# A hybrid attention/RNN decoder layer on 8 cores: gate weights and the first RNN chunk moved across the q,k,v boundary, attention and gating spread over the dense units

## The chip, the cores and the metric

The kernel runs on 8 cores (NeuronCores) of one Trainium2 chip. Each core computes one of the 8 batch elements; the cores exchange nothing. The metric is device time in microseconds of the slowest core. Cores 0 to 3 lie on one die, cores 4 to 7 on the other.

## The reference

One decoder layer, batch 8, 4096 tokens, width 1024, float32 in and out:

```python
h = RMSNorm(x); z = h @ W_in      # q,k,v (512 each) | x_rnn | y_rnn | g_attn | g_rnn (1024 each)
A = moba_attention(q, k, v)       # 8 heads of 64, QK-norm, relative bias,
                                  # own causal block of 256 keys + the top-3 past blocks by q . mean(k)
B = rg_lru(conv1d(x_rnn)) * gelu(y_rnn)
x = x + W_out(sigmoid(g_attn) * (A @ P_attn) + sigmoid(g_rnn) * (B @ P_rnn))
x = x + W_2(relu(RMSNorm(x) @ W_1) ** 2)    # hidden width 4096
```

In the recurrence each channel keeps h_t = a_t h_(t-1) + sqrt(1 - a_t^2) * i_t * conv_t, where a_t and i_t come from two block-diagonal matmuls.

## The kernel before, in words

**Order of the work.** Nothing is issued directly. Helpers `op` (line 461) and `dma` (line 466) append an operation with a modelled cost to a program object `Prog`; afterwards its `schedule` takes, for each engine in turn, the ready operation that comes first in program order, and writes one fixed order per engine. The order in which the Python code calls the helpers is therefore the priority, and tile names (buffers) give the waits. Every compute row of the profile has line 461, every DMA row line 466, so rows are told apart by tile names. PE is the matmul engine, DVE, ACT and POOL do the elementwise work, SP issues the ordinary DMAs. A DMA issued by POOL can convert f32 to bf16 on the way; these are the rows on the queue "software_dynamic".

**Stage A, q,k,v.** 32 tiles of 128 tokens. `FEn(t+1)` normalises a tile and transposes it (`s_hb` to `s_hT`, stored to HBM as `h_s`), `FEm(t)` does 24 matmuls of 128x512 against `s_wqkv`, `FEq(t)` does the QK-norm (`s_ssq` on POOL, `s_qa`, `s_ktm`) and stores q, k, v. From t = 4 one load per tile is taken off the list `wB`, all on POOL's queue with a cast: `wx`, `wy` (8), `wbda`, `wbdi`, then `wga`, `wgr`, `wpr` (12 loads of 512 KB in bf16).

**Stage B, the RNN.** 8 chunks `s` of 512 tokens, each in two halves `g` of four channel tiles. `RNN(s,g)` does 16 matmuls per channel tile with `s_wx`, `s_wy` ("xy"), copies the x half out of PSUM into `s_xr` (ACT), and runs the 4-tap convolution as one ACT and three DVE operations into `s_cv`, then POOL casts to `s_cvb`. The three tokens before the chunk come from a tile `halo`: DVE copies them in and out, two copies of 128x3 per channel tile. `RNN2(s,g)` does the gate matmuls `s_wbda`, `s_wbdi` ("ai"), tanh and exp on ACT, then on POOL the square of a and min(.,1) times -0.25 (a tensor_scalar in place on `s_rr`), the square root on ACT, then products and the scan on DVE, and POOL writes `s_orn`. `GATE1(c,m)` does for one of eight tiles of 128 output channels 8 matmuls each with `s_wga`, `s_wgr` and `s_wpr`, and stores two f32 tiles `t_s` and `rm_s`; four calls for chunk s-1 stand in each half of chunk s. `WCAST` turns two MLP weight slabs per half into bf16 in HBM.

**Stage C.** `QLOAD(c)` loads q of chunk c; `GM(c)` makes, for four tiles of 128 queries, the block mask (matmuls `s_kmBD,s_qp`, top-3 by `s_top`, a transpose of `s_maskb`, then eight small DMAs from `s_mskT` into `s_qT`). `attention(c)` is a list of units, one per head and 128 keys: an S matmul `s_qT,s_kTr` into a PSUM bank, an exp on ACT into `s_PT`, four small matmuls `s_Vr,s_PT`; then transposes into `s_oT`. Attention of chunk 0 alternates with the eight `GATE1(7,m)`. Everything else is a list `dense`: `gating(c)`, eight units of four matmuls `s_oT,s_wpa`, each multiplied (DVE) by the stored gate tile, which SP loads into `s_t1r`, and added to `s_rmr` into `s_mT`; `outproj(c)` with `s_mT,s_wo` and the residual `s_x1T`; and `W1`, `W2` in two halves, `s_h2T,s_wsl` and `s_uT,s_wsl`. `marks[c]` is the position of `gating(c)` in `dense`. The units of `attention(c)` are put among the dense units from `marks[c-1]` to `marks[c]`; `QLOAD(c)` and all of `GM(c)` stand together at `marks[c-1]`. There are two buffers each of `s_t1r` and `s_rmr`.

## Time and profile before

| | us |
|---|---|
| median of 3 runs | 2646.11 (2641.7 to 2646.79) |
| the profiled execution | 2649.26 |
| span of its slowest core, core 3 | 2647.7 |
| spans of the eight cores | 2624.2 to 2647.7 |
| granted TensorE clock, mean of core 3 | 0.953 |

The profile is of core 3. Stage A runs to about 276 us, stage B to about 890 us, attention of chunk 0 to about 1050 us, and the rest is the dense list with attention of chunks 1 to 7 in it. A row of the windows view reads: start and end, length, then for PE, PE's weight loads, DVE, ACT and POOL the busy time (and the number of instructions), then the granted clock of TensorE, the mean busy share of the 16 DMA engines, and GB/s. A clock of 1.00 in these rows is 2.4 GHz; 0.50 would be 1.2 GHz all the time. A row of groups reads: line, engine, operation, out<-in, shapes, count, then busy time and mean ns of one, then the idle time just before them and what ended it. "<-" in a waits row is the thing waited for.

### The profile page before, as it was taken

How to read it: one execution, taken by the hardware profiler on the slowest of the kernel's cores; microseconds unless marked ns; L12 is line 12 of the kernel's file. 1: busy time of each engine (PE TensorE's matmuls, PEld its weight loads, DVE VectorE, ACT ScalarE, POOL GpSimd, SP SyncE). 2: the span in 40 equal slices, each digit the busy share in tenths (PEclk: the TensorE clock that was granted, in tenths of full speed). 3: DMA queues.
4: the chain of work that ended last, by engine and by line, in shares of the span. 5: the costliest groups of instructions: out<-in, count | busy, mean ns of one | idle time of the engine just before them, and what ended most of it. 6: DMA issues, size and time to landing. Idle time of an engine off the chain costs nothing.

```text
span 2647.7 us, 43842 instructions; the slowest of 8 cores (2624.2 to 2647.7 us)
## 1 busy us (share of the span) xinstructions
PE 2369.7 (90%) x14810; PEld 1131.8 (43%) x14810; DVE 1093.7 (41%) x1946; ACT 1287.8 (49%) x2313; POOL 729.4 (28%) x593
## 2 busy tenths in 40 slices
PE   4888689999999776989989989989998998999799
PEld 2444333444444332434434434534543553555344
DVE  3767775866776523233233132133123213211332
ACT  2444666666666523332434434535654664676111
POOL 3665565665565401011011011011001101100110
PEclk9998899999999887999989989999998998999899
DMA  7998555653112445454445455445444544453443
GB/s 189 214 219 168 104 88 128 116 117 93 59 67 72 111 143 161 140 162 163 144 150 180 134 158 150 140 139 163 152 144 147 159 134 129 141 155 113 139 147 127
DMA packets 141364, 367.93 MB, mean 139 GB/s; under 512 B 14867, under 2 KB 49340, under 8 KB 123068
## 3 DMA queue, kind: packets, MB, share of 16 engines
q1 hardware_dynamic: 136492, 331.06, 40.8%
q0 software_dynamic: 4656, 34.08, 9.1%
q8 instruction: 125, 2.05, 0.3%
q14 instruction: 91, 0.75, 0.1%
HBM read 326.73 MB, written 88.16 MB: 157 GB/s over the span
## 4 chain that ended last, share of the span: by engine, by line
PE 69%; issue 8%; DMA 8%; DVE 6%; POOL 3%; ACT 3%; SPq 2%; DVEq 0%; ACTq 0%; POOLq 0%
PE bank L461 69%; DMA q_s<-s_qst 2%; DMA s_t1r<-t_s 2%; SPq L466 2%; POOL s_ssq L461 2%; DVE s_cv L461 1%; DVE s_ii L461 1%; DMA s_xs<-x 1%; DMA s_x1T<-xT 1%; DMA outT<-s_x1T 1%; POOL s_orn L461 1%; ACT L461 1%; ACT s_PT L461 1%; DMA t_s<-s_t_0 1%; DMA rm_s<-s_t_0 1%
## 5 line engine op out<-in xcount | busy, mean ns | idle before, releaser
L461 ACT ACTIVATE s_PT<-bank 128x512 bf16<-128x512 f32 (+3 forms) x1152 | 568.2, 566 | 485.8 <-PE bank L461 482.8
L461 PE MATMUL bank<-s_h2T,s_wsl 128*128 128x512 bf16 x2048 | 520.9, 379 | 2.0 <-ACT s_rl L461 1.3
L461 PE MATMUL bank<-s_uT,s_wsl 128*128 128x512 bf16 x2048 | 508.6, 381 | 4.8 <-DVE s_x1T L461 4.8
L461 PEld LDWEIGHTS bank<-s_Vr,s_PT 128*128 128x128 bf16 x4224 | 251.3, 98 | 284.4 <-issue 223.4
L461 PE MATMUL bank<-s_qT,s_kTr 80*128 80x512 bf16 (+3 forms) x1152 | 359.9, 369 | 9.7 <-DMA s_qT<-s_mskT 7.5
L461 POOL TENSOR_TENSOR s_uT<-s_rl 128x512 bf16<-128x512 f32 x80 | 83.1, 1039 | 985.1 <-ACT s_rl L461 985.1
L461 PE MATMUL bank<-s_Vr,s_PT 128*128 128x65 bf16 x4224 | 313.7, 195 | 23.9 <-ACT s_PT L461 21.7
L461 ACT ACTIVATE s_rl<-bank 128x512 f32<-128x512 f32 x256 | 152.8, 597 | 295.7 <-PE bank L461 294.0
L461 DVE TENSOR_TENSOR s_uT<-s_rl 128x512 bf16<-128x512 f32 x176 | 121.7, 692 | 409.0 <-ACT s_rl L461 408.8
L461 PEld LDWEIGHTS bank<-s_uT,s_wsl 128*128 128x128 bf16 x2048 | 187.1, 98 | 186.1 <-issue 14.2
L461 PEld LDWEIGHTS bank<-s_h2T,s_wsl 128*128 128x128 bf16 x2048 | 183.7, 98 | 165.2 <-issue 3.9
L461 DVE TENSOR_TENSOR s_x1T<-bank,s_x1T 128x512 f32<-128x512 f32 x128 | 88.2, 691 | 396.9 <-PE bank L461 396.9
L461 PE MATMUL bank<-s_wqkv,s_hT 128*128 128x512 bf16 x768 | 190.6, 397 | 10.3 <-DVE s_hbias L461 6.8
L461 DVE SCALAR_TENSOR_TENSOR s_cv<-s_xr,s_pvec,s_cv 128x512 f32<-128x512 f32 x192 | 147.3, 810 | 1.6 <-ACT s_cv L461 1.0
L461 PEld LDWEIGHTS bank<-s_qT,s_kTr 80*128 80x128 bf16 x1152 | 109.1, 99 | 76.5 <-issue 17.3
L461 POOL TENSOR_SCALAR s_rr<-s_rr 128x512 f32<-128x512 f32 x64 | 140.1, 2202 | 0.3 <-POOL s_rr L461 0.3
L461 PE MATMUL bank<-s_hTb,s_wga 128*128 128x512 bf16 x512 | 129.7, 397 | 9.5 <-ACT s_t_0 L461 5.0
L461 PE MATMUL bank<-s_orn,s_wpr 128*128 128x512 bf16 x512 | 124.9, 387 | 8.2 <-POOL s_orn L461 7.1
L461 PE MATMUL bank<-s_mT,s_wo 128*128 128x512 bf16 x512 | 124.7, 385 | 8.0 <-DVE s_mT L461 7.6
L461 PE MATMUL bank<-s_oT,s_wpa 128*128 128x512 bf16 x256 | 91.0, 492 | 44.0 <-DVE s_t1r L461 43.4
L461 POOL TENSOR_TENSOR s_ss<-s_ss,s_sqt 128x512 f32<-128x512 f32 x48 | 60.8, 1266 | 237.4 <-ACT s_sqt L461 219.8
L461 PE MATMUL bank<-s_hTb,s_wgr 128*128 128x512 bf16 x512 | 123.0, 383 | 0.8 <-ACT s_gq L461 0.7
(120 smaller groups left out, 2812.3 us busy)
## 6 DMA issues: line engine op xcount, KB each, us to landing
s_wsl<-wff_s SPq DMA_DIRECT2D x128, 1024.0 KB, 5.3
s_xs<-x SPq DMA_DIRECT2D x32, 512.0 KB, 10.3
wff_s<-wff_p POOLq DMA_DIRECT2D x16, 1024.0 KB, 15.8
s_x1T<-xT SPq DMA_DIRECT2D x64, 256.0 KB, 5.1
s_t1r<-t_s SPq DMA_DIRECT2D x64, 256.0 KB, 3.6
s_rmr<-rm_s SPq DMA_DIRECT2D x64, 256.0 KB, 3.9
outT<-s_x1T SPq DMA_DIRECT2D x64, 256.0 KB, 4.0
h_s<-s_hT SPq DMA_DIRECT2D x32, 256.0 KB, 11.8
```

Source lines behind the costliest of these rows:

```text
L461: return P.add(eng, lambda e, m=meth, kw=kw: getattr(e, m)(**kw), reads, writes, cost=c_, lat=lat, fam=fam, tag=tag or (writes[0] if write ...
L466: return P.add(q, lambda e: e.dma_start(out=out, in_=in_), reads, writes, dsem=dsem, cost=(1000.0 if q == "gpsimd" else 80.0), nbytes=nb, ...
```

## The change

**A to B.** The 12 loads of `wga`, `wgr`, `wpr` leave the per-tile list and are issued at the start of stage B; their tiles now lie over stage A's (`hTb1` over `wqkv0`, `wga` over `wqkv1` and `wqkv2`, `wgr` over `xs`, `wpr` over `hb` and the tiles behind it), so each waits for the last use of what it lies over. `wbda` and `wbdi` come earlier. The first four channel tiles of `RNN(0)` are called in tiles 26 to 29 of stage A, with stage A's banks. `NHT` (buffers of `s_hT`) goes from 6 to 5.

**Within B.** Each channel tile has its own `xr`, so the three tokens are copied inside `xr`, in one DVE copy (a memset in chunk 0), and `halo` is gone. The min moves from POOL to a DVE tensor_scalar on `s_aa`; the factor -0.25 goes into the scale of the square root. The weights `wpa`, `wo` are cast to HBM in chunk 1; the MLP slabs are cast from chunk 2 on.

**B to C.** `oT`, `wpa`, `wo`, `mT`, `t1r`, `rmr` move to a region that stage B leaves early, so their loads can be issued in its end; `wpa` and `wo` are loaded in bf16 by SP. `GATE1(7,m)` uses five banks.

**C.** `GM` is split into one unit per query tile, which stand with `QLOAD` ahead of the heads in `attention(c)`; they use the S banks. `gating(c+1)` stands one unit after each two units of `W1(c,1)`. The attention units of all chunks form one queue that is spread evenly over all dense units up to the last mark; what a gating needs is issued at its mark at the latest.

```diff
+    wpo_s = scr("wpo_s", [128, 12 * D], BF16)
...
+        xr = [alloc("xr%d" % i, [CH + 3], F32) for i in range(8)]
...
-        wB.append((wbda, wbd_d[0], "wbda"))
-        wB.append((wbdi, wbd_d[1], "wbdi"))
-        for p in range(4):
-            wB.append((wga[p], wr_d[2, p], "wga%d" % p))
-            wB.append((wgr[p], wr_d[3, p], "wgr%d" % p))
-            wB.append((wpr[p], wpr_d[p], "wpr%d" % p))
-
+            if p == 1:
+                wB.append((wbda, wbd_d[0], "wbda"))
+                wB.append((wbdi, wbd_d[1], "wbdi"))
+
...
+        def RNN(c, cts, bank):
...
+                if c == 0:
+                    op("vector", "memset", [], ["xr%d:h" % ct], ap=xr[ct][:, 0:3], constant=0.0)
+                else:
+                    op("vector", "tensor_copy", ["xr%d:m" % ct], ["xr%d:h" % ct], out=xr[ct][:, 0:3], in_=xr[ct][:, CH:CH + 3])
...
+                op("vector", "tensor_scalar", ["aa%d" % r], ["aa%d" % r], out=aa[r], in0=aa[r], scalar1=1.0, scalar2=None, op0=ALU.min)
+                op("gpsimd", "tensor_tensor", ["aa%d" % r], ["rr%d" % r], out=rr[r], in0=aa[r], in1=aa[r], op=ALU.mult)
...
+                op("scalar", "activation", ["rr%d" % r], ["rr%d" % r], out=rr[r], in_=rr[r], func=AF.Sqrt, scale=-0.25, bias=0.25)
...
+            if t == 14:
+                HLOAD(0)
+            if 26 <= t < 30:
+                RNN(0, [t - 26], abank)
         st.pop().close()
         cur[0] = baseB
...
+        hTb[1] = alloc("hTb1", [TPC, 8, 128], BF16)
+        wga = [alloc("wga%d" % p, [8, 256], BF16) for p in range(4)]
+        wgr = [alloc("wgr%d" % p, [8, 256], BF16) for p in range(4)]
+        wpr = [alloc("wpr%d" % p, [8, 256], BF16) for p in range(4)]
...
-                op("vector", "tensor_copy", ["halo:%d" % ct, "halo"], ["xr%d:h" % r], out=xr[r][:, 0:3], in_=halo[:, ct, :])
...
-                op("gpsimd", "tensor_tensor", ["aa%d" % r], ["rr%d" % r], out=rr[r], in0=aa[r], in1=aa[r], op=ALU.mult)
-                op("gpsimd", "tensor_scalar", ["rr%d" % r], ["rr%d" % r], out=rr[r], in0=rr[r], scalar1=1.0, scalar2=-0.25, op0=ALU.min, op1=ALU.mult)
...
-                op("scalar", "activation", ["rr%d" % r], ["rr%d" % r], out=rr[r], in_=rr[r], func=AF.Sqrt, scale=1.0, bias=0.25)
...
-        HLOAD(0)
+        for p in range(4):
+            dma("gpsimd", wga[p], wr_d[2, p].rearrange("p (a b) -> p a b", a=8), "wga%d" % p, [], ["wga%d" % p])
+            dma("gpsimd", wgr[p], wr_d[3, p].rearrange("p (a b) -> p a b", a=8), "wgr%d" % p, [], ["wgr%d" % p])
+            dma("gpsimd", wpr[p], wpr_d[p].rearrange("p (a b) -> p a b", a=8), "wpr%d" % p, [], ["wpr%d" % p])
         bias_table2()
         for s in range(NCH):
             for g in range(2):
-                RNN(s, g)
-                if s == 1 and g == 0:
+                if s + g > 0:
+                    RNN(s, range(NR * g, NR * g + NR), dbank)
+                if s == 0 and g == 1:
                     bias_table3()
                 if g == 0 and s + 1 < NCH:
...
-                    WCAST("orn:%d" % ((s * 8 + 4 * g) % NORN))
+                        GATE1(s - 1, m, dbank)
+                if s == 1:
+                    if g == 0:
+                        dma("gpsimd", wpo_s[:, 0:4 * D], wpa_d, "wc0", ["orn8"], ["wpo_s0", "wcq0"])
+                    else:
+                        dma("gpsimd", wpo_s[:, 4 * D:12 * D], wo_d, "wc1", ["orn12"], ["wpo_s1", "wcq1"])
+                if s > 1:
+                    for _ in range(2):
+                        WCAST("orn%d" % ((s * 8 + 4 * g) % NORN))
...
-        assert cur[0] <= endA, (cur[0], endA)
-        NW = 4
-        wsl = [alloc("wsl%d" % i, [4096], BF16) for i in range(NW)]
-        uT = alloc("uT", [16, CH], BF16)
-        cur_w = cur[0]
         oT = [alloc("oT%d" % i, [4, CH], BF16) for i in range(2)]
         wpa = alloc("wpa", [4, D], BF16)
         wo = alloc("wo", [8, D], BF16)
         mT = alloc("mT", [8, CH], BF16)
         t1r = [alloc("t1r%d" % i, [CH], F32) for i in range(2)]
         rmr = [alloc("rmr%d" % i, [CH], F32) for i in range(2)]
+        assert cur[0] <= baseB, (cur[0], baseB)
+        NW = 4
+        wsl = [alloc("wsl%d" % i, [4096], BF16) for i in range(NW)]
+        uT = alloc("uT", [16, CH], BF16)
...
+        def sbank(c):
+            b = SB[sctr[0] % (3 if c >= 1 else 2)]
+            sctr[0] += 1
+            return b
+
+        def GM(c, tl):
...
+            if b >= 3:
+                bk = sbank(c)
+                for hp in range(4):
...
+            bk = sbank(c)
+            op("tensor", "transpose", ["maskb", "identb"], ["B%d" % bk], out=bankb[bk][:, 0:128], in_=maskb, identity=identb)
+            op("vector", "tensor_copy", ["B%d" % bk], ["mskT:%d" % tl], out=mskT[:, tl * 128:(tl + 1) * 128], in_=bankb[bk][:, 0:128])
+            if tl == TPC - 1:
+                for h in range(NH):
+                    dma("sync", qT[s][64:80, h, :], mskT[h * 16:(h + 1) * 16, :], "mk%d" % h, ["mskT:%d" % i for i in range(TPC)], ["qT%d:m%d" % (s, h)])
...
+            units.append((0.0, lambda: QLOAD(c)))
+            units += [(100.0, lambda tl=tl: GM(c, tl)) for tl in range(TPC)]
             for h in range(NH):
                 units += head(h)
...
-                    dma("sync", x1T[:, xi, :], xT_d[dt_ * 128:(dt_ + 1) * 128, c * CH:(c + 1) * CH], "xl%d" % xi, [], [xk])
+                    dma("sync", x1T[:, xi, :], xT_d[dt_ * 128:(dt_ + 1) * 128, c * CH:(c + 1) * CH], "xl%d" % xi, ["oT%d:3" % (c % 2)], [xk])
...
-        QLOAD(0)
-        GM(0)
-        dma("gpsimd", wpa, wpa_d.rearrange("p (a b) -> p a b", a=4), "wpa", [], ["wpa"])
-        dma("gpsimd", wo, wo_d.rearrange("p (a b) -> p a b", a=8), "wo", [], ["wo"])
+        gbank7 = ring([3, 4, 5, 6, 7])
         at0 = attention(0)
+        for _, f in at0[0:5]:
+            f()
+        wpo = wpo_s.rearrange("p (a b) -> p a b", a=12)
+        dma("sync", wpa, wpo[:, 0:4, :], "wpa", ["wpo_s0", "qT0:m7"], ["wpa"])
+        dma("sync", wo[:, 0:4, :], wpo[:, 4:8, :], "wo", ["wpo_s1", "PT2"], ["wo:0"])
+        dma("sync", wo[:, 4:8, :], wpo[:, 8:12, :], "wo", ["wpo_s1", "PT4"], ["wo:1"])
         for m in range(8):
-            for _, f in at0[m * 4:m * 4 + 4]:
+            for _, f in at0[5 + m * 4:9 + m * 4]:
                 f()
-            GATE1(NCH - 1, m)
-        for _, f in at0[32:]:
+            GATE1(NCH - 1, m, gbank7)
+        for _, f in at0[37:]:
...
+        dense.append((6000.0, lambda: None))
         for c in range(NCH):
             nx = c + 1 < NCH
             extend(W1(c, 0))
             extend(W2(c, 0))
-            extend(W1(c, 1))
+            w1 = W1(c, 1)
             w2 = W2(c, 1)
             if nx:
-                marks[c + 1] = len(dense)
-                extend(gating(c + 1))
+                ga = gating(c + 1)
+                for i in range(16):
+                    extend([w1[i]])
+                    if i % 2 == 1:
+                        if i == 1:
+                            marks[c + 1] = len(dense)
+                        extend([ga[i // 2]])
                 o_ = outproj(c + 1)
                 extend(o_[0:4])
                 extend(w2[0:4])
                 extend(o_[4:8])
                 extend(w2[4:8])
             else:
+                extend(w1)
                 extend(w2)
 
-        inject = {}
-        prev = 0
+        queue = []
         for c in range(1, NCH):
-            end = marks[c]
-            at = attention(c)
-            tot = sum(w for w, _ in at)
-            dt_tot = sum(w for w, _ in dense[prev:end])
-            acc = 0.0
-            k = 0
-            inject.setdefault(prev, []).append(lambda c=c: (QLOAD(c), GM(c)))
-            for i in range(prev, end):
-                acc += dense[i][0]
-                goal = tot * min(1.0, acc / (dt_tot * 0.92))
-                while k < len(at) and (sum_ := sum(w for w, _ in at[:k])) < goal:
-                    inject.setdefault(i + 1, []).append(at[k][1])
-                    k += 1
-            while k < len(at):
-                inject.setdefault(end, []).append(at[k][1])
+            for u in attention(c):
+                queue.append((u[0], u[1], c))
+        dcum = [0.0]
+        for w, _ in dense:
+            dcum.append(dcum[-1] + w)
+        tot = sum(q_[0] for q_ in queue)
+        last = dcum[marks[NCH - 1]]
+        acc = 0.0
+        k = 0
+        for i in range(len(dense) + 1):
+            goal = tot * min(1.0, dcum[i] / (last * 0.98))
+            while k < len(queue) and (acc < goal or any(marks.get(c_) == i and queue[k][2] <= c_ for c_ in marks)):
+                acc += queue[k][0]
+                queue[k][1]()
                 k += 1
-            prev = end
-        for i in range(len(dense) + 1):
-            for f in inject.get(i, ()):
-                f()
             if i < len(dense):
                 dense[i][1]()
 
```

What it does to the order, at three places. **PE, end of stage A.** `s_wqkv` marks stage A, `s_wx` and `s_wy` the xy matmuls of stage B, `s_cvb` the gate matmuls of stage B, `s_qa` and `s_ktm` the transposes of the last tiles. Before:

```order
L461 MATMUL bank<-s_hTb,s_wy 128x512 x8
L461 MATMUL bank<-s_hTb,s_wx 128x512 x7
L461 MATMUL bank<-s_identb,s_qa 128x128 x4
L461 MATMUL bank<-s_hTb,s_wx 128x512
L461 MATMUL bank<-s_hTb,s_wy 128x512
L461 MATMUL bank<-s_identb,s_ktm 128x128 x4
L461 MATMUL bank<-s_hTb,s_wy 128x512 x7
L461 MATMUL bank<-s_hTb,s_wx 128x512 x8
L461 MATMUL bank<-s_hTb,s_wy 128x512 x8
L461 MATMUL bank<-s_hTb,s_wx 128x512 x8
L461 MATMUL bank<-s_hTb,s_wy 128x512 x8
L461 MATMUL bank<-s_cvb,s_wbda 128x512
```

With the change:

```order
L462 MATMUL bank<-s_wqkv,s_hT 128x512 x14
L462 MATMUL bank<-s_hTb,s_wy 128x512 x8
L462 MATMUL bank<-s_identb,s_hb 128x128 x8
L462 MATMUL bank<-s_wqkv,s_hT 128x512 x10
L462 MATMUL bank<-s_identb,s_qa 128x128 x4
L462 MATMUL bank<-s_wqkv,s_hT 128x512 x2
L462 MATMUL bank<-s_identb,s_ktm 128x128 x4
L462 MATMUL bank<-s_wqkv,s_hT 128x512 x36
L462 MATMUL bank<-s_identb,s_qa 128x128 x4
L462 MATMUL bank<-s_cvb,s_wbda 128x512
L462 MATMUL bank<-s_cvb,s_wbdi 128x512 x2
L462 MATMUL bank<-s_identb,s_ktm 128x128 x4
```

Before, the 64 xy matmuls of the first half stand between the last `s_wqkv` matmul and the first gate matmul (`s_wbda`); now they stand among the `s_wqkv` matmuls of tiles 26 to 31 (the last eight are the `s_wy` row here), and the first gate matmul follows 36 `s_wqkv` matmuls and a transpose.

**PE, start of stage C.** `s_maskb` is the mask transpose of chunk 0; `s_wga`, `s_wgr`, `s_wpr` are the gate matmuls of chunk 7. Before:

```order
L461 MATMUL bank<-s_orn,s_wpr 128x512 x8
L461 MATMUL bank<-s_hTb,s_wga 128x512 x8
L461 MATMUL bank<-s_hTb,s_wgr 128x512 x8
L461 MATMUL bank<-s_orn,s_wpr 128x512 x8
L461 MATMUL bank<-s_identb,s_maskb 128x128
L461 MATMUL bank<-s_hTb,s_wga 128x512 x7
L461 MATMUL bank<-s_identb,s_maskb 128x128
L461 MATMUL bank<-s_hTb,s_wga 128x512
L461 MATMUL bank<-s_hTb,s_wgr 128x512 x8
L461 MATMUL bank<-s_identb,s_maskb 128x128
L461 MATMUL bank<-s_hTb,s_wga 128x512
L461 MATMUL bank<-s_identb,s_maskb 128x128
```

With the change:

```order
L462 MATMUL bank<-s_orn,s_wpr 128x512 x8
L462 MATMUL bank<-s_identb,s_maskb 128x128
L462 MATMUL bank<-s_hTb,s_wgr 128x512 x6
L462 MATMUL bank<-s_identb,s_maskb 128x128
L462 MATMUL bank<-s_hTb,s_wga 128x512 x8
L462 MATMUL bank<-s_hTb,s_wgr 128x512 x2
L462 MATMUL bank<-s_hTb,s_wga 128x512 x8
L462 MATMUL bank<-s_hTb,s_wgr 128x512 x8
L462 MATMUL bank<-s_hTb,s_wga 128x512 x16
L462 MATMUL bank<-s_identb,s_maskb 128x128
L462 MATMUL bank<-s_orn,s_wpr 128x512 x3
L462 MATMUL bank<-s_identb,s_maskb 128x128
```

Between the second and the third mask transpose 9 gate matmuls stood; now 42 stand there.

**PE, the last boundary in C** (`gating(7)`, with no attention left behind it). `s_h2T,s_wsl` is W1, `s_oT,s_wpa` gating, `s_mT,s_wo` the out projection, `s_uT,s_wsl` W2. Before:

```order
L461 MATMUL bank<-s_identb,s_otm 128x128 x16
L461 MATMUL bank<-s_h2T,s_wsl 128x512 x48
L461 MATMUL bank<-s_oT,s_wpa 128x512 x32
L461 MATMUL bank<-s_mT,s_wo 128x512 x32
L461 MATMUL bank<-s_uT,s_wsl 128x512 x64
L461 MATMUL bank<-s_mT,s_wo 128x512 x32
```

With the change:

```order
L462 MATMUL bank<-s_h2T,s_wsl 128x512 x16
L462 MATMUL bank<-s_oT,s_wpa 128x512 x4
L462 MATMUL bank<-s_h2T,s_wsl 128x512 x16
L462 MATMUL bank<-s_oT,s_wpa 128x512 x4
L462 MATMUL bank<-s_mT,s_wo 128x512 x32
L462 MATMUL bank<-s_uT,s_wsl 128x512 x64
```

The 32 gating matmuls stood in one row behind the last of W1; now four of them follow each 16 matmuls of W1.

## Rows read from the trace of the kernel before

**Rows 1.** The page: busy time by engine, and the chain that ended last.

```profile
PE 2369.7 (90%) x14810; PEld 1131.8 (43%) x14810; DVE 1093.7 (41%) x1946; ACT 1287.8 (49%) x2313; POOL 729.4 (28%) x593
PE 69%; issue 8%; DMA 8%; DVE 6%; POOL 3%; ACT 3%; SPq 2%; DVEq 0%; ACTq 0%; POOLq 0%
```

**Rows 2.** Windows of stages A, B and the start of C, core 3.

```profile
33.00:130.00 97.00, 84.39 (x504) 41.28 (x505) 67.54 (x107) 43.72 (x80) 62.52 (x61) 0.98 0.92 209
130.00:255.00 125.00, 104.83 (x619) 52.75 (x618) 83.59 (x134) 50.97 (x92) 75.52 (x74) 0.90 0.97 199
255.00:276.00 21.00, 19.29 (x127) 10.01 (x126) 17.50 (x31) 9.49 (x16) 12.09 (x10) 1.00 0.71 155
276.00:300.00 24.00, 23.88 (x119) 10.79 (x118) 13.70 (x28) 19.19 (x30) 7.29 (x8) 1.00 0.48 132
300.00:327.00 27.00, 7.80 (x33) 3.16 (x32) 22.90 (x27) 13.12 (x20) 21.86 (x15) 0.68 0.35 39
327.00:375.00 48.00, 41.04 (x170) 17.14 (x169) 36.62 (x56) 34.71 (x51) 30.70 (x24) 0.96 0.58 88
375.00:890.00 515.00, 484.44 (x2191) 215.10 (x2190) 362.33 (x513) 341.38 (x510) 311.11 (x220) 0.98 0.38 92
890.00:1050.00 160.00, 109.04 (x593) 48.63 (x591) 48.74 (x107) 47.80 (x90) 29.37 (x22) 0.80 0.56 158
```

**Rows 3.** Windows of C's chunk boundaries: sixth, seventh, sum of all seven.

```profile
2213.00:2263.00 50.00, 38.28 (x249) 17.21 (x248) 19.23 (x66) 19.27 (x36) 7.88 (x7) 0.83 0.37 128
2463.00:2513.00 50.00, 38.54 (x161) 15.95 (x159) 15.55 (x22) 3.75 (x6) 10.51 (x9) 0.86 0.49 160
sum 350.00, PE 264.67 PEld 119.47 DVE 135.74 ACT 115.98 POOL 59.29; mean PE 37.81 PEld 17.07 DVE 19.39 ACT 16.57 POOL 8.47
```

**Rows 4.** Windows of the longest dense stretch in C.

```profile
2264.00:2460.00 196.00, 194.46 (x1671) 103.06 (x1670) 40.01 (x70) 131.20 (x264) 15.07 (x14) 1.00 0.44 134
```

**Rows 5.** Waits of PE over the span: total, times, longest.

```profile
PE bank L461 <- DVE s_t1r L461: 43.4, 17, 10.9
PE bank L461 <- DVE s_maskb L461: 38.3, 22, 12.2
PE bank L461 <- ACT s_PT L461: 22.9, 42, 2.3
PE bank L461 <- DVE s_hb L461: 19.8, 5, 9.7
```

**Rows 6.** Groups on POOL, 375 to 890 (steady RNN stage).

```profile
L461 POOL TENSOR_SCALAR s_rr<-s_rr 128x512 f32<-128x512 f32 x52 | 114.9, 2221 | 0.2 <-POOL s_rr L461 0.2
```

**Rows 7.** Groups on DVE, 375 to 890.

```profile
L461 DVE COPY s_halo<-s_xr 128x3 f32<-128x3 f32 x52 | 38.2, 735 | 0.0
L461 DVE COPY s_xr<-s_halo 128x3 f32<-128x3 f32 x48 | 5.5, 177 | 0.0
L461 DVE TENSOR_TENSOR s_cv<-s_ii,s_cv 128x512 f32<-128x512 f32 x51 | 37.6, 775 | 0.0
L461 DVE SCALAR_TENSOR_TENSOR s_ii<-s_ii,s_rr 128x512 f32<-128x512 f32 x51 | 72.7, 1463 | 7.0 <-ACT s_rr L461 7.0
```

**Rows 8.** Groups on PE, 375 to 890: the gate matmul wbda.

```profile
L461 PE MATMUL bank<-s_cvb,s_wbda 128*128 128x512 bf16 x52 | 20.8, 401 | 22.4 <-DVE s_xr L461 20.2 <-POOL s_cvb L461 2.2
```

**Rows 9.** Waits of PE, 890 to 1050.

```profile
PE bank L461 <- DVE s_maskb L461: 14.7, 4, 12.2
PE bank L461 <- DVE s_t1r L461: 11.9, 2, 10.9
PE bank L461 <- ACT s_PT L461: 10.1, 17, 2.1
```

**Rows 10.** Groups on DVE, 2213 to 2263 (the sixth boundary).

```profile
L461 DVE SCALAR_TENSOR_TENSOR s_t1r<-s_t1r,bank 128x512 f32<-128x512 f32 x8 | 5.5, 687 | 16.8 <-DMA s_t1r<-t_s 9.3 <-PE bank L461 7.6
```

**Rows 11.** DMA queues (packets, MB, share) and one issue group.

```profile
q0 software_dynamic: 4656, 34.08, 9.1%
s_t1r<-t_s SPq DMA_DIRECT2D x64, 256.0 KB, 3.6
```

193 lines of the change are left out of this document (83 added, 110 removed).

## The prediction, made before the changed kernel ran

> **What bounds the kernel now.** I read the page first: PE is busy for 2369.7 us, 90% of the span, and the chain of waits that ended last lies on PE for 69% [rows 1]. So time can be won only where PE stands idle or runs at the lower clock, and I looked for these places stretch by stretch in the windows view. For each stretch I take two bounds of what is lost: the idle time (length minus PE busy), and the length minus PE busy times the granted clock, since work that ran at a clock under 1.00 would have needed less.
>
> - Stage A, 130 to 255 us: idle 20.2 us, with the clock 30.7 us lost of 125 [rows 2].
> - A to B, 300 to 375 us: idle 19.2 + 7.0 = 26.2 us, with the clock 21.7 + 8.6 = 30.3 us [rows 2].
> - Steady B, 375 to 890 us: 30.6 to 40.2 us of 515 [rows 2].
> - B to C, 890 to 1050 us: 51.0 to 72.8 us of 160 [rows 2].
> - The seven chunk boundaries of C: idle 350 − 264.67 = 85.3 us; with a clock of about 0.85 (0.83 and 0.86 in the two shown) 350 − 225 = 125 us [rows 3].
> - Between the boundaries there is nothing: PE is busy 194.46 of 196 us at clock 1.00 [rows 4].
>
> The list of what PE waited for names the same places: gating's product `s_t1r` 43.4 us, the masks `s_maskb` 38.3 us, `s_hb` of stage A 19.8 us [rows 5].
>
> **The change, part by part.** The sum is made against the profiled execution, 2649.26 us, 3.2 us above the median of 2646.1.
>
> *Loads out of stage A.* From 130 to 255 us the DMA engines are 97% busy and PE loses 16 to 25%. Two neighbours show what is left without the 12 loads: 33 to 130 us, which still carries `wx` and `wy`, loses 12.6 to 14.3 us of 97 (up to 15%), and 255 to 276 us, with DMA at 0.71, loses 1.7 of 21 (8%) [rows 2]. At 15% the 125 us would lose 18.5, a gain of 12; at 8% they would lose 10, a gain of 21. I take −15, for the longest single wait here (9.7 us on `s_hb`, [rows 5]) may come again from x loads alone; ends 0 and −25. NHT 5 instead of 6 costs nothing as long as stores of `s_hT` land within five tiles; if not, the end 0 holds it.
>
> *The start of B.* The first half of `RNN(0)` now stands among the last tiles. Its 64 matmuls are about 64 × 24.0/119 = 12.9 us of PE [rows 2], and they are not saved: tiles 26 to 29 must take them, partly in their idle time. What goes is the stall that follows, since the convolution and casts are done when stage A ends, and the 64 xy matmuls of the second half cover the gates' chain. POOL has 21.86 us of work in those 27 us [rows 2], and four min operations of 2.22 us, 8.9 us, leave POOL [rows 6]. I take −16 of the 26 to 30; ends 0 (DVE, at 17.5 of 21 us at A's end [rows 2], cannot take 4 × 3 convolution steps, and tiles wait) and −28.
>
> The gate weights now land after A ends. POOL's casting queue moved 34.08 MB in 9.1% of 2647.7 us, which is 7.1 us of all engines per MB [rows 11]; the 12 loads are 6 MB, 42 us. By the order of POOL six of them are issued among the last tiles, which leaves 21 us of loads for the time behind stage A. There, two halves of xy, 2 × 12.9 = 26 us of PE, and their gates come before the first matmul with `s_wga`. So the loads are hidden at no cost, but narrowly; the price without that cover is a rival below.
>
> *Steady B.* Per half DVE loses four `s_halo` copies of 0.735 us, 2.9 us, and POOL loses 8.9 us [rows 6, 7]. DVE gains four min operations, which no row shows. Bounds: one input over 128x512 costs no more than the two-input product, 0.775 us, and no less than a small copy, 0.177 us [rows 7]. I take 0.45, between them, which is 1.8 us per half: DVE stays 1 us lighter. The gate matmul waits 20.2 us in all for `s_xr` copies that queue on DVE [rows 8]; with one copy in place of two and chains shorter by the POOL step I take −12; ends +10 (0.775 per min and nothing hidden in half of the halves) and −30.
>
> Here a row and a rule have to be weighed. The two copies of 128x3 take 0.735 and 0.177 us [rows 7]: same size, so the slower is held up by something other than its data, and `s_ii` at 1.463 us against 0.775 for another two-input product shows the same [rows 7]. The Trainium skill, page "SBUF — State Buffer", section "Who interferes with whom", says that DVE copies and tensor_scalars in a two-port mode, and DVE operations with two SBUF inputs against POOL reads, take an exclusive port pair and wait for the whole of a POOL instruction in progress. By that rule the new min, a tensor_scalar, stands in the halo copy's place. In rows: if each of the 64 pays what the slow copy paid over the fast one, 0.56 us, DVE loses 2.2 us per half, and the term for steady B is 0 instead of −12. That is inside its ends.
>
> *B to C.* PE waits 14.7 us for masks, once 12.2, 11.9 us for `s_t1r`, and 10.1 us for `s_PT` [rows 9]. The first `gating` loads and `wpa`, `wo` no longer wait for stage B's end, and 42 gate matmuls (9 us) instead of 9 lie before the third mask transpose. I take the masks' and `s_t1r`'s 26.6 us and half of the lost clock (21.8 us, so 11): −38; ends −15 and −55.
>
> *The boundaries.* In the sixth, DVE waits 9.3 us for the `s_t1r` loads in eight products [rows 10]: eight units of four matmuls in a row use two buffers, and a load takes 3.6 us [rows 11]. With 16 matmuls of W1 (3.5 us) between units, and attention units too, two buffers cover it. The masks are spread likewise. The seventh has no attention and loses as much, 11.5 us idle [rows 3], so the cause is gating, and it gets the same interleaving. Of 85 to 125 us I take −90, ends −50 (the idle time but for the tail into the out projection, 5 us each) and −115.
>
> *The pad of 6000* and the earlier second S bank pair move work, add none: 0.
>
> Sum: −15 − 16 − 12 − 38 − 90 = −171; 2649.3 − 171 = 2478, and 3 less on the median's scale: **2475 us**.
>
> **The rivals.**
> 1. *A and B only move their loss*: the loads collide with other work at B's start, the min takes the copy's place (the rule above), tiles 26 to 29 grow by what is saved later. For it: DVE at 70% in B, DMA at 0.92 even without the 12 loads [rows 2]. Then 2646 − 38 − 90 = 2518. Chance 0.21.
> 2. *The boundaries stay half*: the out projection needs all eight `s_mT`, whose last product comes after the last W1 unit, and `s_x1T` now loads only after `oT`. Then 2475 + 45 = 2520. Chance 0.13.
> 3. *Gate weights late*: 28 us more before the first gate and the start's gain gone: 2475 + 16 + 28 = 2519. Chance 0.05.
> 4. *Slower: the even spread makes PE wait on ACT.* S matmuls, masks and `oT` transposes now share three banks. 1120 units lie in the spread (140 per head); before, a wait for `s_PT` cost 22.9/42 = 0.55 us and came 42 times [rows 5]. It decides from 171/0.55 = 311 units on, 28% of them; at every second unit it costs 305 us: 2780; at a third, 203: 2678. Against it: where attention is densest, PE is 99% busy with ACT at 131 of 196 us [rows 4], and an even spread is thinner. Chance 0.05, at 2678.
> 5. *The change does not do what it says* at the boundaries: what must be issued at a mark is still bunched there, and the troughs stay. Then 2475 + 90 = 2565. Chance 0.05.
>
> **How the numbers follow.** Forecast 2475: 0.51, with 2435 to 2510 of its own. The range of 2425 to 2550 takes in rivals 1 to 3 and most of the forecast's ends, and leaves out rivals 4 and 5 and the far ends. A measurement of this kernel tells about 0.2%, 5 us, from no change. Faster by more: all but rival 4 and a small rest, 0.93; within: 0.02; slower: 0.05.
>
> **What would show it.** Right: the seven windows round the boundaries busy over 47 of 50 us at clock 0.97 or more, the `s_t1r` wait under 10 us; the wait on `s_cvb` after stage A under 5 us; 130 to 255 us losing under 18 us; the B-to-C waits on `s_maskb` and `s_t1r` gone. Wrong: `s_PT` waits in the hundreds (rival 4); a gap before the first `s_wga` matmul with a DMA as its releaser (3); a mean min near 1 us and `s_xr` waits as before (1); waits on `s_mT` or `s_x1T` at each boundary (2).

## The result, and the profile after

The changed kernel takes 2418.8 us (median of 4 runs, 2415.0 to 2421.1) against 2646.3; the ratio is 0.9142, 95% interval 0.9127 to 0.9158. That is 227 us faster where 171 were forecast, and it lies below the range (2425 to 2550). Some executions, of the kernel before too, took some per cent longer, with one or both dies at a lower granted clock; the times of the experiments below are medians of the others, two to seven per kernel. The experiments ran on four chips; the kernel before, run beside them, took 2635 to 2643 us there instead of 2646, so differences of less than about 10 us in the whole are not resolved.

The page, busy time and the chain of waits [rows 1]:

```profile
PE 2294.1 (95%) x14810; PEld 1115.2 (46%) x14810; DVE 1089.0 (45%) x1945; ACT 1272.5 (53%) x2309; POOL 593.8 (25%) x529
PE 80%; DMA 7%; issue 5%; DVE 3%; POOL 3%; ACT 2%; SPq 0%; DVEq 0%; ACTq 0%; POOLq 0%
```

Windows of the changed kernel, core 2, in the columns of [rows 2]; the rows are the second half of stage A, three pieces of B (start, the pause in it, steady), the passage to C, and the dense stretch from the first W1 matmul to the end:

```profile
130.00:255.00 125.00, 117.83 (x730) 59.88 (x728) 103.43 (x165) 66.07 (x114) 81.87 (x77) 0.97 0.94 191
269.00:290.00 21.00, 16.42 (x87) 7.46 (x84) 13.23 (x20) 17.64 (x27) 12.91 (x12) 0.99 1.01 183
290.00:307.00 17.00, 6.21 (x8) 2.34 (x9) 13.00 (x19) 4.98 (x9) 7.91 (x6) 0.60 0.76 123
325.00:806.00 481.00, 472.78 (x2177) 212.38 (x2178) 374.55 (x525) 336.70 (x510) 208.40 (x176) 1.00 0.53 112
806.00:964.00 158.00, 129.57 (x750) 61.57 (x747) 65.30 (x135) 68.55 (x127) 31.30 (x24) 0.87 0.52 169
964.00:2417.00 1453.00, 1428.53 (x10387) 712.96 (x10387) 431.64 (x934) 711.20 (x1411) 172.04 (x150) 1.00 0.51 160
```

From 130 to 255 us 125 − 117.83 × 0.97 = 10.7 us are lost, 30.7 before. Steady B is idle 8.2 of 481 us, 30.6 of 515 before. The dense stretch stands idle for 24.5 of 1453 us at a clock of 1.00; the boundaries have nearly vanished from it.

What PE waited for, over the span [rows 5]:

```profile
PE bank L462 <- ACT s_gq L462: 16.8, 3, 9.5
PE bank L462 <- ACT s_PT L462: 8.0, 15, 1.9
PE bank L462 <- DVE s_maskb L462: 6.7, 4, 3.4
PE bank L462 <- DVE s_t1r L462: 3.6, 2, 2.6
PE bank L462 <- DVE s_mT L462: 2.7, 2, 2.4
PE bank L462 <- POOL s_cvb L462: 0.5, 2, 0.3
```

The wait on `s_t1r` fell from 43.4 to 3.6 us, on `s_maskb` from 38.3 to 6.7, on `s_PT` from 22.9 to 8.0. New is `s_gq` (ACT), 15.4 us of it at B's start, 269 to 325 us. That is core 2; on the other seven cores PE waits there 5.8 to 8.1 us for `s_cvb` and about 7.4 us for `s_gq`.

The stages, read from each core's trace of one profiled execution by the last `s_wqkv`, first `s_wga`, last `s_wx`, first `s_h2T,s_wsl` and last `s_uT` matmul; medians of the eight cores:

| from, to | before | after | change | forecast |
|---|---|---|---|---|
| start to the first gate matmul (A, and B's start) | 275.6 + 75.3 | 268.7 + 54.1 | −28 | −31 |
| to the last xy matmul (steady B) | 512.8 | 477.7 | −35 | −12 |
| to the first W1 matmul (B to C) | 185.8 | 154.5 | −31 | −38 |
| to the end (dense stretch) | 1584.2 | 1449.1 | −135 | −90 |

Two terms came out at about their size, and two were too small: the dense stretch by 45 us, steady B by 23.

### The profile page after: what moved, and what is told of

It reads as the page before. It is cut to its first block, busy times and chain, and to the rows that moved or that the text cites. A ratio compares the mean times of both kernels' runs of the same rounds, so it can differ in the third digit from the quotient of the medians.

```text
span 2416.9 us, 43734 instructions; the slowest of 8 cores (2405.6 to 2416.9 us)
## 1 busy us (share of the span) xinstructions
PE 2294.1 (95%) x14810; PEld 1115.2 (46%) x14810; DVE 1089.0 (45%) x1945; ACT 1272.5 (53%) x2309; POOL 593.8 (25%) x529
## 4 chain that ended last, share of the span: by engine, by line
PE 80%; DMA 7%; issue 5%; DVE 3%; POOL 3%; ACT 2%; SPq 0%; DVEq 0%; ACTq 0%; POOLq 0%
PE bank L462 80%; POOL s_ssq L462 2%; DMA outT<-s_x1T 1%; DMA s_xs<-x 1%; DMA s_qT<-s_mskT 1%; DMA k_s<-s_kst 1%; DVE s_cv L462 1%; DMA s_t1r<-t_s 1%; DMA s_x1T<-xT 1%; DMA t_s<-s_t_0 1%; SPq L467 0%; DMA s_Vr<-v_s 0%; DVE s_ii L462 0%; DVE s_qa L462 0%; ACT s_PT L462 0%
## 5 line engine op out<-in xcount | busy, mean ns | idle before, releaser
L462 PE MATMUL bank<-s_h2T,s_wsl 128*128 128x512 bf16 x2048 | 530.5, 379 | 0.2
L462 DVE SCALAR_TENSOR_TENSOR s_cv<-s_xr,s_pvec,s_cv 128x512 f32<-128x512 f32 x192 | 161.6, 908 | 1.4 <-ACT s_cv L462 1.2
L462 POOL TENSOR_TENSOR s_mT<-s_t1r,s_rmr 128x512 bf16<-128x512 f32 x32 | 40.8, 1276 | 491.2 <-DVE s_t1r L462 317.0
L462 POOL TENSOR_TENSOR s_orn<-s_ii,s_gq 128x512 bf16<-128x512 f32 x64 | 117.6, 1849 | 116.8 <-DVE s_ii L462 107.6
L462 PE MATMUL bank<-s_mT,s_wo 128*128 128x512 bf16 x512 | 132.1, 381 | 3.3 <-DVE s_mT L462 2.7
L462 PE MATMUL bank<-s_hTb,s_wy 128*128 128x512 bf16 x512 | 121.3, 379 | 0.9 <-DVE s_t_1 L462 0.9
## 6 DMA issues: line engine op xcount, KB each, us to landing
s_xs<-x SPq DMA_DIRECT2D x32, 512.0 KB, 10.7
```

Of the source, the lines that this page charges most:

```text
L462: return P.add(eng, lambda e, m=meth, kw=kw: getattr(e, m)(**kw), reads, writes, cost=c_, lat=lat, fam=fam, tag=tag or (writes[0] if write ...
```

## The experiments

"Dense stretch" is the last row of the table above, median of the eight cores of the profiled execution.

**The dense stretch, the two parts one at a time.** In `c_gate_block`, from the changed kernel:

```diff
-                ga = gating(c + 1)
-                for i in range(16):
-                    extend([w1[i]])
...
-                        extend([ga[i // 2]])
+                extend(w1)
+                marks[c + 1] = len(dense)
+                extend(gating(c + 1))
```

> The changed kernel with one part undone: gating(c+1) stands as a block of eight units behind all of W1(c,1), marks there; the even spread of attention and all else stay. The stretch from the first W1 matmul to the end is 1592.6 us before and 1452.8 us with the change. Theory G (the eight gating units in a row, with two buffers, are the cause of the boundary loss, and the loss is larger than idle time plus clock show): 80 to 140 us slower than the changed kernel, 2500 to 2560 us, and PE waits on s_t1r of 30 us or more in all. Rival S (the even spread of attention and masks is the cause; gating was only where the wait showed): under 40 us slower, 2420 to 2460 us, with the eight blocks at a granted clock near 1.

Measured: 2490 us, 71 more than the changed kernel; dense stretch 1512 against 1449. That lies between the ranges of both theories, nearer to G, and the sign that G named failed: PE waits for `s_t1r` 12.2 us over the span, not 30. Two groups on PE from the first W1 matmul to the end show the waits; that on `s_mT` (the tail into the out projection), 13.0 us, is larger than that on `s_t1r`, 8.0:

```profile
L462 PE MATMUL bank<-s_mT,s_wo 128*128 128x512 bf16 x429 | 116.1, 406 | 19.0 <-DVE s_mT L462 13.0 <-DVE s_otm L462 2.9 <-DVE s_m L462 2.4
L462 PE MATMUL bank<-s_oT,s_wpa 128*128 128x512 bf16 x211 | 61.5, 405 | 11.4 <-DVE s_t1r L462 8.0 <-DVE s_mskT L462 2.2 <-DVE s_rcp L462 0.6
```

So the block costs time, but that its two buffers are the reason is not shown: no run has more of them.

In `c_per_chunk` the old injection stands again, without its line for `QLOAD` and `GM`:

```diff
-            goal = tot * min(1.0, dcum[i] / (last * 0.98))
...
+            for i in range(prev, end):
+                acc += dense[i][0]
+                goal = tot * min(1.0, acc / (dt_tot * 0.92))
```

> The changed kernel with another part undone: the units of attention(c), its q load and masks at their head, go among the dense units from marks[c-1] to marks[c] again, in the old way (all placed in the first 92% of that stretch); gating stays interleaved with W1. Theory G: under 40 us slower than the changed kernel, 2420 to 2460 us. Rival S: 60 to 140 us slower, 2480 to 2560 us, with waits on s_maskb and s_PT back at the marks.

Measured: 2415 us, dense stretch 1444. The even spread is worth nothing once gating is interleaved. Rival S falls.

`c_all_old` has both edits, and it makes the four masks of a chunk one unit:

> The changed kernel with the gating block and the injection per chunk both undone; stages A and B and the passage to C stay as changed. If these two edits carry the whole gain of the dense stretch, it takes 120 to 145 us more than the changed kernel, 2540 to 2565 us, whichever theory holds. If its time is under 2520 us, something else in C (three S banks for chunk 1, the masks in S banks, x1T loaded behind oT) carries a part. If the two single undoings sum to clearly less than this one, each edit alone covers for the other.

Measured: 2516 us, dense stretch 1558: 97 us slower, less than the 120 to 145 expected, so something else in C carries a part. The spread does gain 46 us (1558 to 1512, the separate masks included) while gating stands in a block, with attention's units among gating's; interleaving makes it needless.

`before_gate` puts the same interleaving into the kernel before:

```diff
+                ga = gating(c + 1)
+                for i in range(16):
+                    extend([w1[i]])
...
+                        extend([ga[i // 2]])
```

> The kernel before with one part of the change alone: gating(c+1) stands one unit after each two units of W1(c,1), with the mark behind the second; attention is injected from mark to mark, masks stand together at the marks, stages A and B as before. With the rest of the change in place, undoing this part cost 60 to 85 us, and undoing it together with the even spread 97. Theory G (the block of gating is the main cause): 80 to 110 us faster than the kernel before, 2530 to 2560 us. Rival (it pays only where masks and attention are spread too, since the masks at the mark stop PE instead): under 50 us faster.

Measured: 2571 us, ratio 0.974 (0.970 to 0.977); dense stretch 1513, 71 us less, where theory G said 80 to 110. It is the largest single part, but not the 135. What is left between 1513 and 1449 shows in the waits of PE, 1100 to 2600 us:

```profile
PE bank L461 <- DVE s_maskb L461: 24.4, 18, 2.2
PE bank L461 <- DVE s_top L461: 5.7, 12, 0.5
```

**The masks.** `c_masks_bank` leaves the masks where the change puts them and changes the banks alone (the first two lines of the diff, twice). `c_masks_at_mark` also puts them back at the marks (the last line) and injects per chunk; `c_old_masks` is the same with gating in a block:

```diff
-                bk = sbank(c)
+                bk = (gbank() if c >= 1 else sbank(c))
...
+            inject.setdefault(prev, []).append(lambda c=c: (QLOAD(c), [GM(c, tl) for tl in range(TPC)]))
```

> The changed kernel with three parts of stage C undone: the gating block, the injection per chunk, and the masks, which stand together with the q load at marks[c-1] and use the three banks of the dense units again. With the first two undone the dense stretch took about 1559 us, with 1592.6 before. If the masks make the remaining 33 us, 25 to 40 us slower than that kernel, 2540 to 2555 us; if the three S banks for chunk 1 and the late x1T loads make them, within 10 us of it, 2505 to 2525 us.

> The changed kernel with the masks of chunks 1 to 7 standing together with the q load at marks[c-1], in the three banks of the dense units, and the injection per chunk; gating stays interleaved. Against the kernel with the injection per chunk alone (dense stretch 1444 us, median of the cores) only the masks differ. Theory K (the masks at the mark stop PE, and with them gone the last of the boundary's pause goes): the dense stretch 1500 to 1515 us, 2470 to 2490 us in all. Rival X (x1T loads or S banks): within 10 us of 1444, under 2430 us.

> The changed kernel with the masks as units at the head of their chunk's attention, as changed, but in the three banks of the dense units instead of the S banks. Theory K by place: within 10 us of the changed kernel (dense stretch under 1460 us). Theory K by banks (a mask that waits for DVE keeps W1 from a bank): the dense stretch 1480 us or more.

Measured: `c_old_masks` 2532 us, dense stretch 1562, within 4 of `c_all_old` (16 more in the whole, between the two expectations). `c_masks_at_mark` 2458 us, dense stretch 1490, 46 more than with the injection per chunk alone, and 10 under theory K's range. `c_masks_bank` 2458 us, dense stretch 1496, 47 more than the changed kernel. So where gating is interleaved the banks carry all of it; the place of the masks, which the forecast spoke of, adds nothing beside the old banks. Where gating stands in a block, banks and place together are worth 4 us (1562 to 1558). The mask transpose on PE in `c_masks_bank` and in the changed kernel, over the dense stretch:

```profile
L462 PE MATMUL bank<-s_identb,s_maskb 128*128 128x128 bf16 x24 | 6.0, 251 | 20.6 <-DVE s_maskb L462 20.5
```

```profile
L462 PE MATMUL bank<-s_identb,s_maskb 128*128 128x128 bf16 x24 | 5.2, 218 | 1.7 <-DVE s_maskb L462 1.5
```

The reading: in the changed kernel the masks take banks of the S ring, in which attention's units turn over; in the ring of three banks that gating, W1 and W2 use, a mask that waits for DVE's chain (eight `s_top` operations and four more) also holds the order of those units' banks. That the wait goes with the ring is shown, and it makes about 19 of the 47 us; how the planner's order passes it on is my reading.

**Small parts of C.** `c_x1t_early` drops the wait of the x1T loads on `oT`, `c_two_banks` gives chunk 1 two S banks and one O bank, `pool_cost_old` has the planner's old costs of POOL operations:

```diff
-"xl%d" % xi, ["oT%d:3" % (c % 2)], [xk])
+"xl%d" % xi, [], [xk])
...
-            b = SB[sctr[0] % (3 if c >= 1 else 2)]
+            b = SB[sctr[0] % (3 if c >= 2 else 2)]
...
-                    c_ = nel * 1.8 + 150.0
+                    c_ = nel * (2.1 if meth == "tensor_tensor" else 1.05) + 150.0
```

> The changed kernel with the x1T loads free to start before oT is there, as in the kernel before. Theory K: within 10 us of the changed kernel. Rival X (early x1T loads crowd the loads of K, V and W slabs): dense stretch 15 us longer or more.

> The changed kernel with two S banks and one O bank for attention of chunk 1, as before, instead of three and two. If these banks carry the remaining 22 us, the dense stretch takes 1462 us or more against 1449 and the whole 13 to 25 us more; if not, within 6 us.

> The changed kernel with the old modelled costs of POOL operations in the planner (2.1 ns per element of a tensor_tensor and 1.05 of the rest, instead of 1.8 of each), which decide only the order of work. If the order by the new costs carries the remaining 22 us, the dense stretch takes 1462 us or more; if not, within 6 us of 1449 there, and within 10 us in the whole.

Measured: `c_x1t_early` 2429 us, dense stretch 1449, so Rival X falls there; but the passage from B to C takes 166 us instead of 154.5. The `s_x1T` loads there took 12.4 us to land (median), 5.2 in the changed kernel, and PE waits once for a load of V, where it waited 4.8 us (800 to 980 us):

```profile
PE bank L462 <- DMA s_Vr<-v_s: 14.9, 1, 14.9
```

`c_two_banks` 2419 us, dense stretch 1451: nothing. `pool_cost_old` 2421 us, dense stretch 1457: up to 8, between the two expectations.

The account of the dense stretch, 1584 to 1449: gating interleaved −71 (1584 to 1513), the masks' banks −46 (1490 to 1444), the spread +5, and the rest of C's edits −22. That rest is the same in two pairs that differ in gating, 1584 to 1562 and 1513 to 1490; the planner's costs may be 8 of it, and the other 14 stay open. The account holds in this order only: without the masks' new banks interleaving is worth 71 or 72, with them 114 (1558 to 1444).

**Steady B.** `b_min_pool` moves the min back to POOL, `b_halo` brings the halo tile and its second copy back, `b_both_old` does both:

```diff
-                op("vector", "tensor_scalar", ["aa%d" % r], ["aa%d" % r], out=aa[r], in0=aa[r], scalar1=1.0, scalar2=None, op0=ALU.min)
...
+                op("gpsimd", "tensor_scalar", ["rr%d" % r], ["rr%d" % r], out=rr[r], in0=rr[r], scalar1=1.0, scalar2=-0.25, op0=ALU.min, op1=ALU.mult)
...
+                op("vector", "tensor_copy", ["xr%d:m" % ct, "halo"], ["halo:%d" % ct], out=halo[:, ct, :], in_=xr[ct][:, CH:CH + 3])
```

> The changed kernel with the min back on POOL: a tensor_scalar of min and times -0.25 on s_rr, the square root with scale 1. The stretch from the first s_wga matmul to the last xy matmul is 513.9 us before and 480.9 us with the change, 33 us less where 12 were forecast. Theory M (the POOL step of 2.2 us per tile lengthened the gate chain): 20 to 35 us slower, 2440 to 2455 us, with PE waits before the s_wbda matmuls of the halves back. Rival H (the halo copy on DVE did it): under 10 us slower.

> The changed kernel with the halo tile back: two DVE copies of 128x3 per channel tile, one from the tile into s_xr, one from s_xr into the tile behind the convolution, instead of one copy inside s_xr; the min stays on DVE. Theory M (POOL's min made the 33 us of stage B): under 10 us slower than the changed kernel. Rival H (the second copy, queued on DVE, made them): 15 to 35 us slower, with DVE copies of 0.6 to 0.8 us and PE waits before s_wbda.

> The changed kernel with both the min on POOL and the halo copies back. If these two edits carry stage B's gain, 25 to 35 us slower than the changed kernel; if under 15 us, the rest of stage B's gain comes from elsewhere: eight s_xr buffers, the casts of MLP slabs starting a chunk later, or the gates of chunk 0 being loaded in another order.

Measured: `b_min_pool` 2458 us, 39 slower (theory M said 20 to 35), with 28 of it in steady B (505.8 against 477.7, medians of the cores). `b_halo` 2414 us, steady B 483.5: the halo copies cost 6 us there and nothing in the whole. `b_both_old` 2452 us, steady B 508.7; it also gives the second load of `wo` a name of its own. So the min on POOL made 28 of the 35, both edits 31, and 4 stay open. The matmul that waits longest, in the changed kernel (325 to 806 us) and in `b_min_pool` (342 to 850 us):

```profile
L462 PE MATMUL bank<-s_cvb,s_wbda 128*128 128x512 bf16 x52 | 19.7, 378 | 2.3 <-DVE s_t_0 L462 1.9 <-POOL s_cvb L462 0.3
```

```profile
L462 PE MATMUL bank<-s_cvb,s_wbda 128*128 128x512 bf16 x52 | 20.4, 392 | 14.3 <-DVE s_t L462 14.0 <-POOL s_cvb L462 0.3
```

**Stage A and B's start.** `a_late_rnn` calls the first half of `RNN(0)` behind stage A:

```diff
-            if 26 <= t < 30:
-                RNN(0, [t - 26], abank)
...
-                if s + g > 0:
-                    RNN(s, range(NR * g, NR * g + NR), dbank)
+                RNN(s, range(NR * g, NR * g + NR), dbank)
```

> The changed kernel with the first half of RNN(0) called behind stage A instead of in tiles 26 to 29. Forecast for this term was 16 us with ends 0 and 28. Theory E (the early half hides the first convolution chain): 10 to 25 us slower, 2429 to 2444 us, with a wait on s_cvb behind stage A. Rival L (the gates' loads and DVE set the pace behind stage A anyway): within 6 us.

Measured: 2435 us, 16 slower, the size of theory E. Stage A ends earlier (251.1 us against 268.7), the first gate matmul comes 90.7 us later instead of 54.1. But the wait is not the one of theory E: PE waits 4.6 us for `s_cvb` and once 24.7 us for `s_qa`, which DVE could not make, standing still until a store of q had left the buffer `s_qst` (251 to 345 us for PE, 245 to 300 for DVE):

```profile
PE bank L462 <- DVE s_qa L462: 24.7, 1, 24.7
DVE s_qst L462 <- DMA q_s<-s_qst: 25.4, 1, 25.4
```

ACT stands as long for a store of k. Six of the eight cores show such a wait of PE, of 22 to 25 us, and their first gate matmul comes at 340 to 343 us; on the other two, cores 0 and 2, it comes at 322 and 326 us, as in the changed kernel (318 to 326). So the 16 us are what the late stores cost, and where they do not stop the core, the early half is worth nothing that can be seen.

`before_loads_late` takes the 12 loads out of the tiles of the kernel before:

```diff
-            wB.append((wga[p], wr_d[2, p], "wga%d" % p))
...
+                dma("gpsimd", w_, src.rearrange("p (a b) -> p a b", a=8), nm, [], [nm])
```

> The kernel before with one part of the change alone: the 12 loads of wga, wgr, wpr are taken out of the tiles and issued by POOL at the start of stage B, into their own region as before; no RNN work is moved. Theory D (these loads starve stage A): 12 to 25 us faster in stage A, and the loads land before the first gate matmul 75 us later, so 2621 to 2634 us. Rival T (x loads keep the DMA engines full anyway, or the loads are late in B): within 6 us of the kernel before, or slower.

Measured: 2688 us, ratio 1.016 (1.011 to 1.022), slower by about 45 us. The edit was not the one meant. Without a read to wait for, the planner issued the loads at the very start; the row gives the shortest, middle and longest issue in ns, and the first and last start in us, and the window behind it is 33 to 130 us, where PE stood idle for 40 us (12.6 before [rows 2]):

```profile
L466 POOL DMA_DIRECT2D s_wga<-wr_p x4: 547/574/588, 9.1 to 34.1; - x4
```

```profile
33.00:130.00 97.00, 57.01 (x285) 26.91 (x286) 39.37 (x64) 24.85 (x44) 33.21 (x35) 0.85 0.89 182
```

`before_loads_paced` holds them to the last tile:

```diff
-                dma("gpsimd", w_, src.rearrange("p (a b) -> p a b", a=8), nm, [], [nm])
+                dma("gpsimd", w_, src.rearrange("p (a b) -> p a b", a=8), nm, ["hT%d" % ((NT - 1) % NHT)], [nm])
```

> The kernel before with the 12 loads of wga, wgr, wpr issued by POOL when the last tile's hT is there, and not, as in the kernel tried first, at the very start. Theory D (these loads starve stage A between 130 and 255 us): stage A 12 to 25 us shorter; at B's start POOL has 12 issues of 0.6 us and 42 us of transfers, so the first gate matmul may come 0 to 15 us later: 2620 to 2640 us against about 2641. Rival T (x loads alone keep the DMA engines full): stage A ends within 5 us of 276 us, and the kernel is not faster.

Measured: ratio 0.995 (0.993 to 0.997), 14 us faster. Stage A shrinks by 24 us (275.6 to 251.8, medians of the cores), and from 130 to 254 us DMA is at 0.78 instead of 0.97:

```profile
130.00:254.00 124.00, 115.92 (x750) 60.07 (x751) 102.33 (x165) 62.96 (x111) 86.49 (x77) 1.00 0.78 175
```

B's start gives 11 back (86.3 us to the first gate matmul, 75.3 before): the wait on `s_cvb` behind POOL, before (276 to 375 us) and now (250 to 345), is

```profile
PE bank L461 <- POOL s_cvb L461: 19.7, 2, 19.2
```

```profile
PE bank L461 <- POOL s_cvb L461: 28.3, 1, 28.3
```

It is not POOL's twelve issues that delay the casts: the last is made at 263 us, and the wait lies from 285 to 314 us. POOL stands still ahead of its first `s_orn`, which it writes before these casts, until a store of k out of stage A has landed (250 to 330 us):

```profile
POOL s_orn L461 <- DMA k_s<-s_kst: 15.9, 1, 15.9
```

On all eight cores this stop lasts 11.5 to 16.1 us; five of them name that store. The stores of k took up to 42.7 us to land there, up to 9.4 before, with the DMA engines at 0.95 to 1.06 from 254 to 307 us. So the price of loading late is that stage A's last stores land late, here as in `a_late_rnn`. In the changed kernel the stores of q and k took up to 21.5 us, and POOL still stands 7 to 9 us for one of q on four of the cores.

**A version meant to beat both.** `start_order` loads the identity and QK-norm weights first and computes B's constants at tile 10; `start_per_chunk` adds the injection per chunk.

```diff
+        dma("sync", identb, cid_d, "c0a", [], ["identb"])
+        dma("sync", qkcol, qk_d, "c0e", [], ["qkcol"])
         load_x(0)
         dma("sync", nw, nw_d, "c0b", [], ["nw"])
-        dma("sync", identb, cid_d, "c0a", [], ["identb"])
...
+            if t == 10:
+                setup()
```

> A version meant to beat the changed kernel: the identity and the 1 KB of QK-norm weights are loaded ahead of x, and the small constants of stage B (nsp, hbias) are computed at tile 10 instead of at the start, where PE waits 16.3 us for the identity and 5.9 us for hbias. If those waits end last there, 5 to 12 us faster than the changed kernel, 2407 to 2414 us. If the three loads of wqkv end last, within 3 us of it.

> Both edits that measured no worse than the changed kernel together: the identity and the QK-norm weights first and the constants of stage B at tile 10 (8 us less in the runs of that edit alone), and the injection of attention per chunk (dense stretch 1444 us against 1449). Expected 2402 to 2412 us; if the injection is worth nothing, 2408 to 2414.

Measured: 2411 us (0.913, 0.911 to 0.915) and 2406 us (2403.4 to 2408.8; 0.910, 0.906 to 0.915). Both beat the kernel before. All four runs of the second lie under the lowest of the changed kernel, 2415.0, but the intervals overlap, and by the stages it takes what `c_per_chunk` takes, 2398 us in sum against 2404 of the changed kernel; a gain over the changed kernel is not shown. The reason given for the first edit did not hold: in the window 0 to 33 us of `start_per_chunk` PE is no busier (4.58 us, 5.59 in the changed kernel), it waits for the next tile instead of the identity, and its first `s_wqkv` matmul comes at 26.5 us instead of 18.3. Stage A's end, 263.0 us in `start_order` and 266.1 in `start_per_chunk`, is no sign either: it lies at 264 to 266 us in the runs that change stage C alone.

## Why the prediction was wrong

- **The boundaries: the failed step, in size.** I bounded the loss by seven windows of 50 us, 85 to 125 us, and took −90; measured is −135, of which interleaving made 71 and the masks' banks 46. First, the loss was larger than these windows hold, since I had read "nothing" for all that lies between them from one stretch: over the whole dense stretch (medians of the cores) 101.5 us idle and 35.7 us of clock, 137, of which 22.6 remain. Second, "busy" hides some: the time that PE was busy there, with what ran at the lower clock counted half, fell from 1448 to 1427 us for the same work. So what went is 115 us of idle time and clock and 20 us of such busy time. One part of the 20 can be estimated: eight 128x512 matmuls in a row take 1.89 us and a single one 0.38, so records overlap, and at a stop about 0.16 us of the last record counts as busy that otherwise lies under the next; PE's busy time there has 122 pieces before and 29 after (slowest cores), which makes about 15 us. The rest stays open. The gating matmuls of that stretch, before and after, show the wait that went; that their busy time fell from 77.1 to 60.1 us is the clock, as one at full clock takes 379 ns before and 378 after:

```profile
L461 PE MATMUL bank<-s_oT,s_wpa 128*128 128x512 bf16 x224 | 77.1, 479 | 31.5 <-DVE s_t1r L461 31.5
```

```profile
L462 PE MATMUL bank<-s_oT,s_wpa 128*128 128x512 bf16 x224 | 60.1, 378 | 0.0
```

  So "length minus busy times clock" was not an upper bound. Third, the tail that my end of −50 kept, 5 us per boundary, did not stay: PE waits 2.7 us for `s_mT` in all.
- **The masks' banks: a line I did not price, inside the same term.** "The masks are spread likewise" costed the place, and the place was worth nothing; the ring of banks was worth 46 us. I read the diff's `gbank` to `sbank` as a move that adds nothing.
- **Steady B: the second failed step, −12 forecast and −35 measured.** The mechanism I weighed, two copies against one, was worth 6 us. The POOL step, which I named only beside it ("chains shorter by the POOL step"), was worth 28. My price of the min, 0.45 us, was low: it takes 0.806 us in the mean, above the upper end of 0.775, and DVE got no lighter (374.55 us busy in 481, against 362.33 in 515 [rows 2]). But another operation got faster, `s_ii` from 1463 to 944 ns (groups on DVE, 325 to 806 us):

```profile
L462 DVE SCALAR_TENSOR_TENSOR s_ii<-s_ii,s_rr 128x512 f32<-128x512 f32 x54 | 48.8, 944 | 9.4 <-ACT s_rr L462 9.4
L462 DVE TENSOR_SCALAR s_aa<-s_aa 128x512 f32<-128x512 f32 x52 | 40.0, 806 | 87.2 <-ACT s_aa L462 87.2
L462 DVE COPY s_xr<-s_xr 128x3 f32<-128x3 f32 x48 | 8.5, 242 | 0.0
L462 DVE SCALAR_TENSOR_TENSOR s_cv<-s_xr,s_pvec,s_cv 128x512 f32<-128x512 f32 x156 | 134.2, 931 | 0.0
```

  With the min back on POOL, the same operation takes 1281 ns (342 to 850 us):

```profile
L462 DVE SCALAR_TENSOR_TENSOR s_ii<-s_ii,s_rr 128x512 f32<-128x512 f32 x54 | 67.1, 1281 | 8.3 <-ACT s_rr L462 8.3
```

  The rule of the Trainium skill, page "SBUF — State Buffer", section "Who interferes with whom", gave 0 for this term; measured is −35. The rows agree with the rule in kind, that a two-input DVE operation is slower while POOL works: of the 54 `s_ii` of the changed kernel's steady B, the 26 with no POOL operation beside them took 688 ns and the others 1182, and before only 1 of 52 had none beside it. The new min obeys it too, as I had weighed: 14 of 52 stood alone and took 427 ns, near my 0.45, the others 946. I had applied it to the operation that was added and not to the one that was removed: 52 POOL operations of 2.2 us left the pair of engines. But not all of DVE's operations gained: the three convolution steps per tile take 931 ns where they took 798 (375 to 890 us):

```profile
L461 DVE SCALAR_TENSOR_TENSOR s_cv<-s_xr,s_pvec,s_cv 128x512 f32<-128x512 f32 x156 | 117.8, 798 | 0.1
```

  Per tile the gate chain lost 2.2 us on POOL and 0.34 on `s_ii` (1281 to 944) and gained 0.81 for the min; how much of the 28 us each makes is not separated by a run.
- **Stage A and the start: right in size** (−28 of −31), in part by luck. The loads out of the tiles gave 24 in the kernel before, where I took 15, and took 11 back at the start, where I took nothing: the stores that land late were no term of mine. The early half was worth 16 as forecast, but by keeping clear of these stores and not by hiding the convolution's chain. The gate weights were not late (rival 3): no load of them appears among PE's waits behind stage A. The wait on `s_cvb` fell from 19.7 us to 0.5 on core 2 and to 5.8 to 8.1 on the others, not under the 5 that I had named there, and waits for `s_gq` came up beside it.
- **B to C: right in size** (−31 of −38), with waits that shrank and did not go: on `s_maskb` from 14.7 to 5.2 us, on `s_t1r` from 11.9 to 3.6, and 9.5 us on loads of K and V came up (806 to 964 us). Late x1T loads, which I costed at nothing, carry 12 of it.
- **The other rivals.** 4 fell: `s_PT` waits 8.0 us, less than before. 2 and 5 fell: 20 us of idle time are left in the whole dense stretch, 101.5 before. 1 fell: A and B gained 63 us.
